# Feed-forward slabs of 8, 8 and 6 instead of 6, 8 and 8, the last one run group by group

## The reference, cut to what matters

```python
# DEPTH 4, BATCH 8, SEQ 2048, D_MODEL 1024, D_FF 2816; x is (BATCH, SEQ, D_MODEL)
for l in range(DEPTH):
    proj = x @ w_in[l]
    ya = short_gated_conv(...)      # 3 taps along the tokens, gated, 384 channels
    yb = multiscale_pool(...)       # trailing means over 2, 4, 8, 16 tokens, 256 channels
    yc = chunked_sgu(...)           # gelu, LayerNorm per head, 128x128 token mixing, 384 channels
    mix = concat([ya, yb, yc]) @ w_o[l]
    h = layer_norm(ALPHA * x + mix, ln1_g[l], ln1_b[l])
    g, u = split(h @ w_gate_up[l])  # 2816 columns each
    x = layer_norm(ALPHA * h + (silu(g) * u) @ w_down[l], ln2_g[l], ln2_b[l])
```

## Time and profile before

| | |
|---|---|
| median of 3 runs | 2636.99 us (2636.37 to 2637.74) |
| the profiled execution | 2636.52 us, span 2634.7 us (1.8 us lie around the span) |
| spans of the 8 cores | 2627.0 to 2634.7 us |
| PE busy | 2565.3 us, 97% |
| DVE, ACT, POOL busy | 1314.1, 747.6, 406.8 us |

### The profile page before, as it was taken

The page is one execution under the profiler, slowest core; times in us unless marked ns, Lnnn a source line. Parts: engine busy times, 40 slices in busy tenths (PEclk is TensorE's granted clock), DMA queues, the critical chain, the costliest instruction groups (busy, mean ns, idle before and its releaser), DMA issues.

```text
span 2634.7 us, 36696 instructions; the slowest of 8 cores (2627.0 to 2634.7 us)
## 1 busy us (share of the span) xinstructions
PE 2565.3 (97%) x12320; PEld 1176.5 (45%) x12320; DVE 1314.1 (50%) x2441; ACT 747.6 (28%) x1273; POOL 406.8 (15%) x673
## 2 busy tenths in 40 slices
PE   6999999999999999999999999999999999999997
PEld 3444444444444444444444444444444444444443
DVE  4767331314987632231687754222178774413229
ACT  3534101012653401101365340110146433010112
POOL 3421000000442100000144110000015411000001
PEclk9999999999999999999999999999999999999999
DMA  7644422032455523222254443322226534321303
GB/s 169 130 71 73 80 47 41 13 60 40 80 90 96 92 49 56 40 41 34 44 94 88 83 81 53 59 33 48 37 45 105 102 67 78 59 33 24 56 9 128
DMA packets 162933, 173.00 MB, mean 66 GB/s; under 512 B 126272, under 2 KB 128448, under 8 KB 162752
## 3 DMA queue, kind: packets, MB, share of 16 engines
q0 software_dynamic: 32960, 113.39, 25.7%
q1 hardware_dynamic: 129792, 57.28, 10.2%
HBM read 246.27 MB, written 8.39 MB: 97 GB/s over the span
## 4 chain that ended last, share of the span: by engine, by line
PE 92%; DVE 2%; issue 2%; POOL 2%; ACT 1%; DMA 1%; DVEq 0%; POOLq 0%; ACTq 0%; SPq 0%
PE P L665 46%; PE P L700 23%; PE P L494 13%; PE P L651 8%; PE P L509 2%; POOL SM L524 1%; DMA W<-w_v 1%; DVE X L465 0%; POOL T L604 0%; DVE T L591 0%; DMA X<-x 0%; POOL SM L523 0%; PE P L550 0%; ACT VN L537 0%; PE P L620 0%
## 5 line engine op out<-in xcount | busy, mean ns | idle before, releaser
L665 PE MATMUL P<-XT,W 128*128 128x512 bf16 x5632 | 1217.5, 379 | 0.0
L665 PEld LDWEIGHTS P<-XT,W 128*128 128x128 bf16 x5632 | 551.0, 98 | 664.5
L670 DVE TENSOR_TENSOR BIG<-P,E 128x512 bf16<-128x512 f32 x352 | 243.4, 691 | 870.7 <-PE P L665 852.8
L700 PE MATMUL P<-W,BIG 128*128 128x512 bf16 x2816 | 609.7, 379 | 0.0
L669 ACT ACTIVATE E<-P 128x512 f32<-128x512 f32 x352 | 209.9, 596 | 1287.4 <-PE P L665 1287.4
L476 DVE SCALAR_TENSOR_TENSOR X<-X,P 128x512 f32<-128x512 f32 x512 | 346.8, 686 | 277.8 <-PE P L700 234.5
L494 PE MATMUL P<-XT,W 128*128 128x512 bf16 x1792 | 413.7, 387 | 25.9 <-DVE T L618 5.6
L700 PEld LDWEIGHTS P<-W,BIG 128*128 128x128 bf16 x2816 | 275.5, 98 | 332.3
L494 PEld LDWEIGHTS P<-XT,W 128*128 128x128 bf16 x1792 | 175.3, 99 | 239.9 <-issue 45.0
L651 PE MATMUL P<-W,BIG 128*128 128x512 bf16 x1024 | 222.3, 379 | 0.0
L463 ACT ACTIVATE JUNK<-X,MVB 128x1024 bf16<-128x1024 f32 x128 | 146.4, 1144 | 114.3 <-DVE MVB L461 111.8
(11 more groups left out here) (62 smaller groups left out, 964.5 us busy)
## 6 DMA issues: line engine op xcount, KB each, us to landing
W<-w_gu_t POOLq DMA_DIRECT2D x88, 512.0 KB, 6.7
W<-w_chunks POOLq DMA_DIRECT2D x56, 512.0 KB, 7.1
W<-w_dn_t POOLq DMA_DIRECT2D x44, 512.0 KB, 5.2
X<-x SPq DMA_DIRECT2D x16, 512.0 KB, 10.5
W<-w_o_t POOLq DMA_DIRECT2D x16, 512.0 KB, 7.5
out<-X SPq DMA_DIRECT2D x16, 512.0 KB, 2.6
W<-w_v POOLq DMA_DIRECT2D x16, 384.0 KB, 5.7
GBUF<-ln_g SPq DMA_DIRECT2D x8, 512.0 KB, 3.8
```

The costliest lines, as they stand in the source:

```text
L665: r = e.matmul(o.handle[:], lhsT=wv[:, h, k, :], rhs=XT[:, k, n * 512:(n + 1) * 512], start=(k == 0), stop=(k == 7))
L670: S.add("dve", lambda e: e.tensor_tensor(out=BIG[:, ml, n * 512:(n + 1) * 512], in0=pu.handle[:], in1=t.handle[:], op=ALU.mult), reads=[pu ...
L700: r = e.matmul(pv.handle[:], lhsT=BIG[:, kk, i * 128:(i + 1) * 128], rhs=w[:, kk % 2, nh * 512:(nh + 1) * 512], start=(kk == 0), stop=(kk ...
```

## The change

The slabs become 8, 8 and 6. The first goes through the groups outermost as before, with the `catch_up` normalisations after every second block of the first two groups. The second is as before. The last slab (6 blocks) also goes through the groups outermost, and its down products are taken out of the final loop: after gate/up of group n come the down products, residual additions and normalisations of the four tiles of group n-1; those of the last group come at the end. For that all six gate/up weights and the three down weights of the slab must be resident at once: two of the down weights go into blocks 6 and 7 of `BIG`, which a slab of 6 does not use. The scheduler gets a chain `heir`/`follow` that keeps all ring loads on POOL in the order of the program.

```diff
@@ order() @@
-            op.npred = len(op.deps)
+            op.npred = len(op.deps) + op.follow
...
+            if op.heir is not None:
+                op.heir.npred -= 1
+                op.heir.ready = max(op.heir.ready, start + dur)
...
-SLABS = ((0, 6), (6, 8), (14, 8))
+SLABS = ((0, 8), (8, 8), (16, 6))
...
+        for k in (6, 7):
+            S.pool(f"W{k}", [BIG[:, k, :]])
...
+            if wlast:
+                wlast[-1].heir = o
+                o.follow = True
...
+                if last:
+                    wd = [wload(w_dn_d[l, (m0 + kk) // 2], spare=(6, 7, None)[kk // 2]) for kk in range(0, nm, 2)]
+                if si != 1:
+                    for n in range(NG):
+                        for ml in range(nm):
+                            gate_up(ws[ml], ml, n)
+                            if si == 0 and n < 2 and ml % 2:
+                                catch_up([("BIG", ml - 1, 4 * n)])
+                        if last and n > 0:
+                            for t in range(4):
+                                down(wd, nm, 4 * n - 4 + t, si, after)
+                if not last:
+                    wd = [wload(w_dn_d[l, (m0 + kk) // 2]) for kk in range(0, nm, 2)]
+                for i in range(12 if last else 0, NT):
+                    down(wd, nm, i, si, after)
```

58 lines of the change are left out of this document (29 added, 29 removed).

## The result

The changed kernel takes 1.0089 times the kernel before, with an interval of 1.0071 to 1.0108, some 23.5 us: about 2660, where 2636.8 was forecast, with a range of 2623 to 2650. Executions of it in which one die was disturbed are left out. The profiled execution took 2664.42 us with a span of 2662.7.

The account below looks back on a forecast made before the run. PE was taken to bound the kernel, busy 2565.3 of 2634.7 us. Boundary waits -2.4, clock 0 and tail +2.2 summed to -0.2 us, so 2636.99 became 2636.8 us, range 2623 to 2650.

Parts of the forecast that it names:

- Feed-forward 0: Feed-forward, all layers: same matmuls in another order, 0 us, since gate/up matmuls between down blocks let DVE catch up.
- Weights 0: Weight loads of feed-forward and boundary: all land in time, cost 0, margin 2 us by the worse landing figure.
- Tail +2.2 by the walk: Behind PE's end: walking the new order with measured durations gives a tail of 19.5 us instead of 17.3, +2.2 us.
- First wait +3.4: Each of three boundaries: PE waits 5.7 us instead of 2.25 for the first convolution's last tap, +3.4 us each.
- upper bound of 9.4: First wait at a boundary: 9.4 us if ACT's two squares and a cast, 3.7 us, add up.
- the five instructions: DVE at each boundary: five more instructions in front of the last tap, 3.65 us, moving its end to 32.4 us.
- Second waits -4.0: Each of three boundaries: the later waits of 1.57 and 2.47 us go, -4.0 us each, 4.6 in the third.
- Clock 0: PE's clock at each boundary: the 1.75 us lost to a slow clock stay, only earlier, 0 us.
- forecast of -0.2: Whole kernel: waits -2.4, clock 0 and tail +2.2 us give a total of -0.2 us.
- The slower rival: Boundaries' second half: POOL becomes late, PE waits 3 to 4 us again, +12 us, 2649 us; slower outcome's chance 0.26.

Follow-up runs that it names:

- e3: Changed kernel, but the last slab runs all gate/up products block by block, with all down products behind them; 1.0304 of the kernel before.
- e15: Kernel before in layers 0 to 2, the new feed-forward in the last layer only; 1.0013 of the kernel before.
- e7: Changed kernel, next layer's LayerNorm loads held to the mixers' last third, second half's chunk weights loaded to a quarter of their columns; 1.0043 of the kernel before.
- e13: Changed kernel with PE, DVE, ACT and POOL tied at each boundary to the order of the kernel before, LayerNorm steps included; 1.0012 of the kernel before.
- e12: Changed kernel with PE, DVE and ACT tied at each boundary to the order of the kernel before, LayerNorm steps included; 1.0056 of the kernel before.
- e5: Changed kernel with PE and DVE tied at each boundary to the order of the kernel before, LayerNorm steps included; 1.0046 of the kernel before.
- e16: Changed kernel with three instructions moved at each boundary: two POOL clearings behind powers, one ACT copy later; 1.0094 of the kernel before.
- e11: Changed kernel, only the second half's seven chunk weight loads cut to a quarter of their columns; 1.0049 of the kernel before.

## Why the prediction was wrong, step by step

Two steps failed. The sum had no term for the transpositions that move with the normalisations, and they cost 12 us of the 23.5. And the waits of the boundaries were forecast to cancel (+3.4 and -4.0), where they measured +4.8 and -1.9 at the first boundary of core 4.

**Feed-forward 0: right.** On core 7 of after the last 26 us in front of PE's end, down products in a row, are full; the line below it is the tail:

```profile
2617.00:2643.00 26.00, 26.00 (x122) 11.62 (x119) 18.32 (x41) 6.96 (x11) 3.10 (x4) 1.00 0.11 44
2643.20:2662.70 19.50, 0.00 (x0) 0.00 (x0) 14.37 (x26) 3.97 (x8) 3.18 (x4) 0.63 0.38 153
```

The cover held; e3, which takes it away, shows the waits that it prevented, 3.7 us.

**Weights 0: right.** The largest wait of core 7 for a chunk weight is 1.4 us, where the text allowed 1.

**Tail +2.2 by the walk (19.5 us): right.** 19.6 us on cores 4 and 7, 19.8 in e15.

**First wait +3.4: right in kind, too small, and one wait was missed.** Forecast was one wait of 5.7 us, ended by the last tap; there are two, 7.0 to 7.6 us together, inside the upper bound of 9.4. The step that failed is "what it waits for is the end of the last tap". The second thing that PE wants there, VN of tile 7 for group 1's token mixing, was not priced, although the order showed that mixing moved. The tap's own wait, 3.6 to 4.2 us, is then less than 5.7, since PE comes to it later by the first wait. Mis-sized by 1.3 to 1.9 us a boundary. The tap's end moved from 28.7 to 34.1 us behind the feed-forward, 5.4 us where 3.65 were counted: the five instructions are there, but DVE also begins the mixers 1.1 us later than before (4.6 instead of 3.5), for which the text had no term.

**Second waits -4.0: about half wrong.** On core 4 there remain 2.1 us at the first boundary and 3.3 at the second. I had taken DVE to be "done 10 us or so before PE asks", from sums over queue work. It is not: the pooled buffers (L627) still release PE, 1.49 us at 100 us behind the feed-forward. Sums over one queue's work leave out that queue's own waits for the others; which of them used up the 10 us is not shown.

**Clock 0: right, for the regular part.** On core 4 the boundary without its idle time is 180.9, 180.0 and 181.4 us, before 181.2, 181.0 and 181.2. Behind the wait of 11.8 us the clock is at its lower level, 1.2 GHz (core 7):

```profile
1420.00:1425.00 5.00, 0.00 (x0) 0.00 (x0) 2.46 (x10) 0.00 (x0) 0.00 (x0) 0.50 1.64 50
1425.00:1430.00 5.00, 1.68 (x5) 0.60 (x6) 0.00 (x0) 0.00 (x0) 0.00 (x0) 0.50 0.76 132
```

and eight matmuls last 3.57 us instead of 1.89. That agrees with the Trainium skill ("TensorE: Matmul & The Clock Gate", section "HAM oscillation — how this bites in real kernels"), where a wait for a DMA brings the array back at half rate.

**The sum with the measured sizes** (core 4, first boundary): the first waits +4.8 (7.0 less 2.25), the second ones -1.9 (2.1 less 4.04), so +2.9 at a boundary, +9 at three, and +11 with the tail. e7, which has the regular part alone, measures 1.0043, 11.3 us. The forecast of -0.2 was 11 us off there. The slower rival priced +12 at the boundaries, but for another reason: a POOL queue in the second half. There is no wait of that size there: those that end with a power (L537) in the second half reach 2.3 us on one core over all three boundaries. What the order of POOL's whole queue is worth, e13 against e12 shows.

**Missed outright: the transpositions, +12 us.** The part on weights looked at the loads that PE wants, and the moved normalisations were priced on DVE, ACT and POOL. No term was given to the transpositions that move with them on SP's queue. The earlier trace rows already had the warning: 11.7 us for a load where several and the transposes meet.

**What stays open.** The regular part is bound to the four queues' order as a whole (e13, e15), and its waits are named. Which places carry it isn't settled: e5 and e12 leave 1.0046 and 1.0056, e16's three moves give nothing. That the transposition is slowed by bytes in flight is shown (e7, e11); why PE waits for `XT` on two cores of eight and not on the others is not. No run has the old slab sizes with the last slab group by group, so how much of the boundaries' loss the sizes alone would bring is open too. The `heir` chain is no cause: without it `Sched.order` gives every engine the same stream.

## What to carry to other kernels

A stage in which PE never waits has nothing to give, and rewriting it re-plans everything behind it: of a re-planned list price every operand of each moved product, not only the releaser that stood there before, and every DMA that moves with a moved step, by what is in flight at its new time. Where queues on five engines feed each other in a circle, removing one visible wait moves it; test a cause by putting back one engine's whole order after the other. And look at all cores: a loss on one of them only can have another cause than the loss on all.

## What the hardware showed unexpectedly

- A transposing DMA lands 3.1 us after its issue at its fastest (minimum and median on core 7 of e7) and up to 22.0 us beside 512 KB weight loads at a boundary, 26.2 inside the feed-forward. The issue of one held the queue 10.7 us instead of 1.2, and with it all that SP had to issue next; and its source buffer stayed taken, so that ACT waited too.
- A DVE step with two inputs in SBUF took 0.56 us, and 1.42 us while POOL ran an addition (L617, 691.02 to 692.48). DVE's timeline of after, core 4:

```profile
687.15 0.56 DVE L540 TENSOR_TENSOR S<-S,SM 128x384 f32<-128x384 f32 x1
...
691.47 1.42 DVE L540 TENSOR_TENSOR S<-S,SM 128x384 f32<-128x384 f32 x1
```

  Over all eight cores this step (L540) took 1.42 us in the 8 places where L617 ran beside it and 0.54 to 0.56 us in the other 248, also where a power ran beside it from before its start to behind its end. The same core, POOL and DVE:

```profile
704.67 1.32 POOL L537 TENSOR_TENSOR SM<-SM,CNH 128x6 f32<-128x6 f32 x1
```

```profile
704.93 0.56 DVE L540 TENSOR_TENSOR S<-S,SM 128x384 f32<-128x384 f32 x1
```

  This was seen, not tested by a run. The 1.42 us agree with the Trainium skill ("SBUF — State Buffer", section "Who interferes with whom"), by which such a step and POOL's reads share a port; the steps beside a power did not wait as that section would have it.
